# A fused five-layer network on one core: first weight block in two transfers, x rounded first and squared last

## The reference

```python
def rms_norm(x, g):
    xf = x.astype(jnp.float32)
    y = xf * lax.rsqrt(jnp.mean(xf * xf, axis=-1, keepdims=True) + RMS_EPS)
    return (y * g.astype(jnp.float32)).astype(x.dtype)
...
        z = rms_norm(x, norm_mix[l]) @ w_in[l]
```

## Time and profile before

| what | us |
|---|---|
| median of 3 runs | 3137.42 |
| lowest and highest run | 3136.39, 3138.01 |
| the profiled execution | 3140.82 |
| its span, first to last instruction | 3139.0 |
| TensorE busy in the span | 3095.1 (99%) |
| VectorE, ScalarE, GpSimd busy | 1418.4, 1275.0, 1506.0 |
| first product starts | 9.28 |

### The profile page before, as it was taken

One profiled execution on the slowest core, in us unless ns is written; L12 is line 12 of the kernel. 1 busy time (PEld: TensorE's weight loads), 2 busy tenths in 40 slices (PEclk: granted clock), 3 DMA queues, 4 the chain that ended last, 5 costly groups with the idle time before them and its releaser, 6 DMA issues.

```text
span 3139.0 us, 35691 instructions
## 1 busy us (share of the span) xinstructions
PE 3095.1 (99%) x14211; PEld 2463.5 (78%) x14211; DVE 1418.4 (45%) x2640; ACT 1275.0 (41%) x1972; POOL 1506.0 (48%) x738
## 2 busy tenths in 40 slices
PE   8999999999999999999999999999999999999999
PEld 5667888875788887778888888888888887588887
DVE  5564111188633346445343554423534358753433
ACT  5463222256443344554333333323433336643432
POOL 3224544566354453334555534443455557545554
PEclk9999999999999999999999999999999999999999
DMA  5212333344232333222323322222232325333222
GB/s 187 78 41 88 101 94 97 98 122 129 77 104 89 101 101 104 91 81 89 106 91 98 96 91 81 77 84 74 89 106 91 98 98 136 103 96 101 90 98 87
DMA packets 89894, 303.11 MB, mean 97 GB/s; under 512 B 10112, under 2 KB 10368, under 8 KB 89600
## 3 DMA queue, kind: packets, MB, share of 16 engines
q1 hardware_dynamic: 89152, 299.77, 31.0%
q10 hardware_dynamic: 576, 1.06, 0.1%
HBM read 281.42 MB, written 2.10 MB: 90 GB/s over the span
## 4 chain that ended last, share of the span: by engine, by line
PE 88%; DVE 7%; ACT 1%; DMA 1%; SPq 1%; issue 0%; POOL 0%; ACTq 0%; DVEq 0%; POOLq 0%
PE PS L1448 26%; PE PS L1450 26%; PE PS L1449 26%; DMA PT<-PD 1%; DVE XL L2049 1%; DVE XH L2047 1%; PE PS L1634 1%; PE PS L1471 1%; PE PS L1462 1%; PE PS L1460 1%; PE PS L1461 1%; DVE PS L2327 1%; PE PS L1475 1%; DVE X L2059 1%; PE PS L1527 1%; DVE TT L2054 1%
## 5 line engine op out<-in xcount | busy, mean ns | idle before, releaser
L2485 POOL TENSOR_TENSOR WL<-RAW,WH 128x1024 fp32r<-128x1024 f32 x504 | 1213.8, 2410 | 1251.0 <-ACT WH L1738 1250.8
L1448 PE MATMUL PS<-XH,WH 128*128 128x512 f32 x2640 | 1057.7, 401 | 13.4 <-POOL WL L2485 11.9
L1450 PE MATMUL PS<-XH,WL 128*128 128x512 f32 x2640 | 1030.8, 390 | 0.0
L1449 PE MATMUL PS<-XL,WH 128*128 128x512 f32 x2640 | 1030.1, 390 | 0.0
L1738 ACT ACTIVATE WH<-RAW 128x1024 fp32r<-128x1024 f32 x504 | 529.2, 1051 | 451.8 <-PE PS L1450 439.1
L1448 PEld LDWEIGHTS PS<-XH,WH 128*128 128x128 f32 x2640 | 496.8, 188 | 150.1 <-issue 42.7
L1449 PEld LDWEIGHTS PS<-XL,WH 128*128 128x128 f32 x2640 | 497.3, 188 | 107.1 <-issue 8.6
L1450 PEld LDWEIGHTS PS<-XH,WL 128*128 128x128 f32 x2640 | 496.8, 188 | 106.0
L1448 PE MATMUL PS<-HH,WH 128*128 128x512 f32 x1264 | 495.4, 392 | 8.5 <-DVE HL L2370 4.4
L1449 PE MATMUL PS<-HL,WH 128*128 128x512 f32 x1264 | 493.7, 391 | 0.0
L1450 PE MATMUL PS<-HH,WL 128*128 128x512 f32 x1264 | 493.5, 390 | 0.0
(11 more groups left out here) (259 smaller groups left out, 2379.4 us busy)
## 6 DMA issues: line engine op xcount, KB each, us to landing
RAW<-wst SPq DMA_DIRECT2D x504, 512.0 KB, 3.5
PT<-PD SPq DMA_DIRECT2D x32, 260.0 KB, 5.0
BI<-natb SPq DMA_DIRECT2D x16, 384.0 KB, 4.4
PT<-PD SPq DMA_DIRECT2D x20, 258.0 KB, 4.8
X<-xin SPq DMA_DIRECT2D x16, 256.0 KB, 4.8
PT<-PD SPq DMA_DIRECT2D x8, 262.0 KB, 4.7
X<-cmpw SPq DMA_DIRECT2D x1, 2048.0 KB, 8.3
out<-X SPq DMA_DIRECT2D x8, 256.0 KB, 2.0
```

The lines of the kernel that those rows point to most:

```text
L1448: e.matmul(o, wh, h, start=first, stop=False)
L1449: e.matmul(o, wh, l, start=False, stop=False)
L1450: t = e.matmul(o, wl, h, start=False, stop=last)
L2485: e.tensor_tensor(WL[:, b % NSPLIT, :], RAW[:, b % NRAW, :], WH[:, b % NSPLIT, :].bitcast(f32), SUB).then_inc(*did(lo_made, ("lo", b)))
```

## The change

The parameters' first part is fetched by ScalarE's queue and a table load (`tables`) put right behind it. Weight block 0 arrives in two transfers of 512 columns; the first half is split by ScalarE and VectorE (event `lo_first`, tiles 0 to 3), the second by ScalarE and GpSimd. Block 1 is fetched between x chunks 4 and 5, block 2 behind chunk 7. ScalarE rounds all eight chunks first, with the splits of blocks 0, 1 and 2 behind chunks 0, 4 and 7, and squares them last; VectorE adds all squares, in a PSUM bank. GpSimd adds none. TensorE starts with five float32 products of 256 columns of a tile that VectorE has cleared. `linear` gets `held=1`: the statistics and the evacuation of m0 come behind m1 instead of behind m0. The core of the diff:

```diff
+            step("fetch_act", PRM[:, 0:n1], prm[:, 0:n1], prm_in, "prm", ())
+            step("tables")
             fetch(X[:, 0, :], xin[0, :, :], x_in[0], ("x", 0))
+            fetch(RAW[:, 0, 0:512], wst[0, :, 0:512], first_in, "raw_first")
             load_block()
             for k in range(1, 8):
                 fetch(X[:, k, :], xin[k, :, :], x_in[k], ("x", k))
+                if k == 4:
+                    load_block()
+            load_block()
...
+            def linear(mv, mc, evac, mid=None, pace=0, wide=False, late=0, held=0):
                 kc = len(mv)
+                waiting = []
                 if wide:
                     first_wide(mv, evac, mid, late)
                 for m in range(WIDE if wide else 0, mc):
@@ -357,13 +362,18 @@
                         done = mac(bank, mv, k, kc)
                         if pace and k % pace == pace - 1:
                             flush_ready()
-                    if m == 0 and mid is not None:
+                    waiting.append((m, bank, done))
+                    if m < held:
+                        continue
+                    if m == held and mid is not None:
                         mid()
                     if not pace:
                         flush()
                     while (bg or soon) and len(tiles.spare) < ROOM:
                         next_step()
-                    evac(m, bank, done)
+                    for group in waiting:
+                        evac(*group)
+                    waiting.clear()
...
+            def first_chunk(n, k):
+                i = step("first_chunk", k, n["gain"](k), ("x", k))
+                n["mv"].append((XH[:, k, :], XL[:, k, :], (i, "lo")))
+
+            def first_squares(n):
+                bank, n["sq"] = banks.get(), tiles.get()
+                for k in range(8):
+                    s = tiles.get() if k else bank
+                    i = step("first_square", k, s.ap, s.free, bank.ap, n["sq"].ap, n.get("sum"))
+                    if k:
+                        s.done((i, "sum"))
+                    n["sum"] = (i, "sum" if k else "sq")
+                bank.done(n["sum"])
...
+            z, bank = tiles.get(), banks.get()
+            cleared = step("clear", z.ap, ())
+            i = step("warm", bank.ap, (), z.ap[:, 0:128], z.ap[:, 0:256], (cleared, "zero"), 5)
+            bank.done((i, "mm"))
+            z.done((i, "mm"))
             for k in range(8):
-                norm_chunk(norm, k, ("x", k), "prm", first=True)
+                first_chunk(norm, k)
                 if k == 0:
+                    step("split_first")
+                if k in (0, 4, 7):
                     split_block()
+            first_squares(norm)
...
-            linear(norm["mv"], 22, mix_evac, mid=lambda: norm_stats(norm), pace=1)
+            linear(norm["mv"], 22, mix_evac, mid=lambda: norm_stats(norm), pace=1, held=1)
...
+                w.wait_ge(*at("lo_first" if b == 0 and j < 4 else ("lo", b)))
...
+                    t = e.matmul(bank[:, 0:x.shape[1]], h, x, start=True, stop=True)
...
+            def split_first(i):
+                w.wait_ge(*at("raw_first"))
+                e.activation(WH[:, 0, 0:512], RAW[:, 0, 0:512], ACT.Copy).then_inc(*did(hi_made, "hi_first"))
...
+                if b == 0:
+                    e.activation(WH[:, 0, 512:1024], RAW[:, 0, 512:1024], ACT.Copy).then_inc(*did(hi_made, ("hi", 0)))
+                    return
...
+            def first_square(i, k, s, s_free, bank, sq, total):
+                for event in s_free:
+                    w.wait_ge(*at(event))
+                e.activation(s, X[:, k, :], ACT.Square).then_inc(*did(act_made, (i, "sq")))
...
+                e.tensor_tensor(WL[:, 0, 0:512], RAW[:, 0, 0:512], WH[:, 0, 0:512].bitcast(f32), SUB).then_inc(
+                    *did(dve_made, "lo_first"))
...
+            def first_square(i, k, s, s_free, bank, sq, total):
+                if k:
+                    w.wait_ge(*at((i, "sq")))
+                    w.wait_ge(*at(total))
+                    e.tensor_tensor(sq if k == 7 else bank, bank, s, ADD).then_inc(*did(dve_made, (i, "sum")))
...
+                if b == 0:
+                    e.tensor_tensor(WL[:, 0, 512:1024], RAW[:, 0, 512:1024], WH[:, 0, 512:1024].bitcast(f32),
+                                    SUB).then_inc(*did(lo_made, ("lo", 0)))
+                    return
...
-            def norm_chunk(i, k, gain, x_made, first, s, s_free, sq, total):
-                if first and k % 2:
-                    w.wait_ge(*at((i, "sq")))
-                    w.wait_ge(*at(total))
-                    e.tensor_tensor(sq, sq, s, ADD).then_inc(*did(pool_made, (i, "sum")))
```

More of the change, by code:

```diff
@@ L390, in new_norm, with norm_chunk @@
                 return {"gain": lambda k: pcol(name, first + k), "mv": [], "z": None}
-            def norm_chunk(n, k, *x_made, first=False):
+            def norm_chunk(n, k, *x_made):
                 s = tiles.get()
@@ L395, in norm_chunk @@
                     n["sq"] = s
-                i = step("norm_chunk", k, n["gain"](k), x_made, first, s.ap, s.free, n["sq"].ap, n.get("sum"))
+                i = step("norm_chunk", k, n["gain"](k), x_made, s.ap, s.free, n["sq"].ap, n.get("sum"))
                 n["mv"].append((XH[:, k, :], XL[:, k, :], (i, "lo")))
@@ L943, in keep_warm @@
                 bank = banks.get()
-                i = step("warm", bank.ap, bank.free, n)
+                i = step("warm", bank.ap, bank.free, ones, mask[:, 0:T], "cst2", n)
                 bank.done((i, "mm"))
@@ L1666, in singles, with warm @@
                     e.matmul(bk, dgs[j], pad[:, j:j + T], start=j == 0, stop=False)
-            def warm(i, bank, free, n):
+            def warm(i, bank, free, h, x, made, n):
                 for event in free:
                     w.wait_ge(*at(event))
-                w.wait_ge(*at("cst2"))
+                w.wait_ge(*at(made))
                 for _ in range(n):
-                    t = e.matmul(bank, ones, mask[:, 0:T], start=True, stop=True)
+                    t = e.matmul(bank[:, 0:x.shape[1]], h, x, start=True, stop=True)
                 t.then_inc(*did(pe_made, (i, "mm")))
@@ L1742, in split_to, with norm_chunk, first_chunk @@
                 e.activation(HH[:, k, :], src, ACT.Copy).then_inc(*did(act_made, (i, "hi")))
[L1744 removed]
+            def norm_chunk(i, k, gain, x_made, s, s_free, sq, total):
                 for event in x_made:
                     w.wait_ge(*at(event))
[L1747 to L1749 removed]
                 for event in s_free:
                     w.wait_ge(*at(event))
[L1752 removed]
+                e.activation(s, X[:, k, :], ACT.Square).then_inc(*did(act_made, (i, "sq")))
+            def first_chunk(i, k, gain, x_in):
+                w.wait_ge(*at("prm"))
+                w.wait_ge(*at(x_in))
+                e.activation(XH[:, k, :], X[:, k, :], ACT.Copy, scale=gain).then_inc(*did(act_made, (i, "hi")))
+            def first_square(i, k, s, s_free, bank, sq, total):
+                for event in s_free:
+                    w.wait_ge(*at(event))
+                e.activation(s, X[:, k, :], ACT.Square).then_inc(*did(act_made, (i, "sq")))
             def rsqrt(i, rs, rs_free, acc, made, mat, n, bank, bank_free):
@@ L2040, in clear, with norm_chunk @@
                 e.memset(o, 0.0).then_inc(*did(dve_made, (i, "zero")))
-            def norm_chunk(i, k, gain, x_made, first, s, s_free, sq, total):
+            def norm_chunk(i, k, gain, x_made, s, s_free, sq, total):
                 x = X[:, k, :]
[L2044 to L2047, removed]
+                for event in x_made:
+                    w.wait_ge(*at(event))
+                e.tensor_scalar(XH[:, k, :], x, gain, None, MUL).then_inc(*did(dve_made, (i, "hi")))
                 w.wait_ge(*at((i, "hi")))
@@ L2050, in norm_chunk @@
                     *did(dve_made, (i, "lo")))
-                if k and not (first and k % 2):
+                if k:
                     w.wait_ge(*at((i, "sq")))
@@ L2054, in norm_chunk, with split_first, first_chunk @@
                     e.tensor_tensor(sq, sq, s, ADD).then_inc(*did(dve_made, (i, "sum")))
+            def split_first(i):
+                w.wait_ge(*at("hi_first"))
+                e.tensor_tensor(WL[:, 0, 0:512], RAW[:, 0, 0:512], WH[:, 0, 0:512].bitcast(f32), SUB).then_inc(
+                    *did(dve_made, "lo_first"))
+            def first_chunk(i, k, gain, x_in):
+                w.wait_ge(*at((i, "hi")))
+                e.scalar_tensor_tensor(XL[:, k, :], X[:, k, :], gain, XH[:, k, :].bitcast(f32), MUL, SUB).then_inc(
+                    *did(dve_made, (i, "lo")))
+            def first_square(i, k, s, s_free, bank, sq, total):
+                if k:
+                    w.wait_ge(*at((i, "sq")))
+                    w.wait_ge(*at(total))
+                    e.tensor_tensor(sq if k == 7 else bank, bank, s, ADD).then_inc(*did(dve_made, (i, "sum")))
             def add_x(i, m, bank, made):
```

(3 more changed lines are left out.)

18 lines of the change are left out of this document (9 added, 9 removed).

## The result

The changed kernel took 3145.89 us in the median of nine executions, the kernel before, nine executions too, 3138.01: slower by 7.9 us, a ratio of 1.0024 with a 95% interval from 1.0015 to 1.0033. The prediction was 3135.7, in a range from 3132.5 to 3140.0. The span of the profiled execution is 3144.1 us against 3139.0. These two differ by 5.1 only, because the profiled execution of before lay 2.8 us above its median; at equal places of the order the two traces are 8.3 us apart near 60 us and 8.0 near 191 us.

What follows compares the result with a forecast made beforehand. TensorE, busy 99% of the span, was the bound, with early waits for GpSimd's weight remainders. m2 starts 8.4 us early, VectorE's chain after the statistics leaves 1.7: 3137.42 - 1.7 = 3135.7 us, range 3132.5 to 3140.0.

Steps and rivals of the forecast that it cites:

- What takes it back: After the statistics, VectorE's fixed order makes TensorE wait, cutting m2's 8.4 us earlier start to 1.7 us gained.
- The mark: Start of to_tokens (transposes) of m3 on TensorE, full from there; forecast 44.15 against 45.88 before.
- I take it that VectorE goes on: In the opening, VectorE subtracts chunk 7 before GpSimd takes block 2, a lead of 0.15 us; XL 7 at 14.6.
- rival 1: In the opening, GpSimd takes block 2 before chunk 7: XL 7 at 16.9, 0.6 slower, 3138.0; chance 28 in a hundred.
- the literal reading: Shared SBUF access in the opening: GpSimd's earlier request wins by the documented rule, so XL 7 ends at 16.9.
- the early ends: Landings of weight blocks in the opening: block 1 at 9.3 and block 2 at 12.6, taken for the forecast.
- the late ends: Later landings of weight blocks in the opening: block 1 at 9.8 and block 2 at 13.0, not taken.
- One block falls into that stretch now, so one such wait: VectorE's tail before the mark: one wait for GpSimd instead of two, 7.8 us instead of 8.67, end 22.1.
- And from there TensorE is full as before: Behind the mark, TensorE never waits, so the 1.7 us gained there stays to the end.
- Rival 3: Clock falls while TensorE waits from tile 5: m0 and m1 slowed 2.5 us, 3138.2 or worst 3140.5; 12 in a hundred.

Runs made afterwards that it cites:

- e8: Changed kernel without the five products of the cleared tile and without the clearing; 3146.16 us, ratio 1.0025 to the kernel before.
- e2: Changed kernel with the split of weight block 2 put behind the eight squares instead of behind chunk 7's rounding; 3141.46 us, ratio 1.0013 to before.
- e4: Changed kernel with held=1 taken out, so statistics and evacuation of m0 stand behind m0 again; 3141.96 us, ratio 1.0007 to before.
- e5: Changed kernel with the edits of e1, e2 and e3 together; 3137.47 us, ratio 0.9996 to before.
- e1: Changed kernel with four idle float32 products on TensorE right ahead of the transposes of m3; 3140.98 us, ratio 1.0006 to before.
- e11: Kernel before with held=1 alone, statistics and evacuation of m0 behind m1; 3149.71 us, ratio 1.0037 to before.
- e3: Changed kernel with forget_log due after 5 tiles instead of 6, its reciprocal ahead of q's head_gain; 3144.24 us, ratio 1.0017 to before.
- e7: Changed kernel, new opening: x fetched ahead of block 1, splits of blocks 1 and 2 later, statistics five tiles into m1, gates later; 3132.94 us, ratio 0.9982.
- e9: The kernel of e7 once more, in more rounds; 3133.10 us, ratio 0.9984 to the kernel before.
- e10: The kernel of e7 without the five products of the cleared tile and without the clearing; 3133.25 us, ratio 0.9985 to the kernel before.

## Why the prediction was wrong

**What held.** The structure did. The bound moved from weights to the chain of statistics and VectorE, as the part "What takes it back" has it. From the logarithm (25.13) the evacuation of m2 ended 14.3 us on and k's product started 15.0 us on, against 14.3 and 14.9 forecast. The waits named there appeared in order, 1.46, 0.79, 1.48 and 4.05 for 1.6, 0.95, 2.4 and 2.2. Of the cleared tile's products the prediction said that they lie where nothing was to do; e8 shows that they also bring nothing.

**The mark, forecast at 44.15, came at 48.76.** Three terms make up the 4.6 us.
- "I take it that VectorE goes on" was the wrong side of the toss: GpSimd took block 2 before chunk 7 and held it until 17. That was rival 1, priced at 2.3, with the earlier request served first, as the literal reading beside the forecast had it; e2 measured 2.2 (5.81 against 3.66).
- The landings. Block 1 landed at 10.2 and block 2 at 13.4, 0.85 later than the early ends that I took; the late ends would have been 0.4 off. 0.86 us:

```profile
RAW<-wst SPq DMA_DIRECT2D x1, 512.0 KB, 6.2
...
RAW<-wst SPq DMA_DIRECT2D x1, 512.0 KB, 7.3
```

(issues at 4.02 and 6.14).
- "One block falls into that stretch now, so one such wait": two fell, at 41.13 and 43.90, the second on the scan (2.61 against 1.22 before). 1.5 us.

With these the sum would have been 2.9 slower, 3140.3. The other 5.4 us of the 8.3 between the traces are the clock.

**"And from there TensorE is full as before" was the step that failed most.** It was full, but at half the clock from 49 to some 61 us, and that cost 5.4 us. Rival 3 knew that the clock falls in a long wait and had the row for it, and looked for the place in the opening, between chunks 4 and 5. The wait ahead of the mark stood in the prediction's own chain with 2.2 us, and no bound was put on it. It was 4.05: counted from the logarithm VectorE was done 23.6 us on instead of 22.1, by the second block, and TensorE was there 19.6 us on instead of 19.9. (From m3 on the order is not quite as before: k's product stands behind the sixth tile of m3 and no longer the fifth, and so five tiles lie between it and the mark where the prediction counts six.) Rival 1 moved the mark but not this wait: in e2, without it, the wait was 4.04. The opening's place was real too: behind the wait for chunk 5 the clock fell in e2, e4 and e5. In the changed kernel it fell earlier, behind the wait of 1.73 us for chunk 1 (low from 9.3 to 12.7), and there VectorE hid it. e1 is the proof of the price: 5 us back for filling the wait. Rival 3 at its worst was put at 3140.5, and the chance of more than 0.2% slower at 0.02; both left out that a late end of VectorE's tail moves the mark and lengthens the wait ahead of it at once, so that the two costs come together.

**Where the gain went.** The change ended TensorE's waits for weights, and m2 does start right behind the statistics' product, near 25 us instead of 30.11. But one group of work in hand was bought with statistics that come 4.2 us later. From the statistics to the mark 24.75 us pass in the changed kernel and in e8, 24.76 in e1, e2 and e11, whenever the statistics start; 26.0 before and 26.2 in e4, where they stand behind m0. Another order on VectorE shortened it to 22.3 in e3 and e5, and the new opening to 20.6 in e7 and e9 and 20.7 in e10. e11 prices a group held back in the kernel before at 11.8 us, with the statistics' product 9.1 us late.

## What to carry to other kernels

When a change removes waits from the busiest engine, follow the slower engine's fixed order to the next place where the two meet, and put bounds on the wait there too: a wait of 4 us costs itself and then the clock behind it. Held-back statistics are not free because their consumer has other work: with them behind m1, the same 24.8 us passed between them and the mark in every kernel that kept the rest of VectorE's order. The version with 0.9982 starts them in the middle of a group, 2.8 us earlier than the change (21.23 against 24.01), but that is still 1.4 later than before. It is faster than before because the stretch behind them is 5.4 us shorter (20.6 against 26.0): its VectorE takes the reciprocal ahead of q's `head_gain`, as in e3, and only one subtraction falls on the tail. It changes several things at once, and no run tells what each is worth. Look at how long a wait is before products are put into it: 3.4 us of them won 5 us in a wait of 4.05, and cost about 1.8, by the estimate above, in one of 1.65. And where VectorE and GpSimd meet on tiles in SBUF, whole instructions of 2.4 us change places with a few tenths of lead, so a forecast should carry both orders all the way through.

## What the runs showed of the hardware that was not expected

The clock's fall has a price that varies between kernels with the same wait: 3.2 us in e3, 4.3 in e8, 5.4 to 5.6 in the others, behind waits of 4.01 to 4.06 us. In the opening the clock fell behind shorter waits too. Behind waits for chunk 5 of 2.92 (e5), 3.00 (e2) and 3.36 us (e4) it did; behind 2.66 us in e3 it did not. It fell behind 1.42 and 1.73 (e1 and the changed kernel, ahead of chunk 1), 1.80 (e1, ahead of chunk 7) and 2.12 and 2.24 (e7 and e9, ahead of block 1), and it did not behind 1.78 (the changed kernel, ahead of chunk 7). So the length of the wait alone does not tell it here.

The granted clock of a window did not show the low level that a kernel started at. In e8, without the cleared tile's products, the window from 10 to 20 us reads 1.00, but until 14.3 the products of a tile start every 0.43 us, as they do at the low level, and every 0.23 from there on:

```profile
10.00:20.00 10.00, 7.95 (x27) 5.62 (x26) 8.54 (x8) 9.18 (x14) 4.90 (x3) 1.00 1.04 408
...
12.37 0.63 PE L1477 MATMUL PS<-XH,WL 128*128 128x512 f32 x1
12.80 0.63 PE L1475 MATMUL PS<-XH,WH 128*128 128x512 f32 x1
...
15.16 0.40 PE L1475 MATMUL PS<-XH,WH 128*128 128x512 f32 x1
15.39 0.39 PE L1476 MATMUL PS<-XL,WH 128*128 128x512 f32 x1
```

In the kernel before the window from 10 to 15 us reads 1.00 too, with a product every 0.43 us until 14.5. So the 0.84 of e7 and 0.83 of e9 in that window against the 1.00 of e10 do not show that the cleared products cost clock later: e10 was at the low level until 10.8, and its wait for block 1 was 0.81 us where e7 and e9 waited 2.12 and 2.24. The medians of e9 and e10 are the same within 0.2 us.
